# Down projections: the first four weight halves listed in TensorE's order; in the even layer the index weights become 16 more columns of the key tile

## The reference, cut to what matters

```python
x = x + (silu(gate) * val) @ w_down          # 2816 hidden -> 1024, in all four layers
```

```python
qa, ka, va, qb, kb, vb, qi, ki, wi = split_cols(h @ w_in_even[j], sizes_even)
...
rel = relu(einsum('bqhd,bsd->bqhs', qii, rmsnorm(ki)) * (64 ** -0.5))
score = einsum('bqhs,bqh->bqs', rel, wi * (16 ** -0.5))
```

## Time and profile before

| | |
|---|---|
| time, median of 3 runs | 1575.7 us (1574.05 to 1576.84) |
| profiled execution: its time, its span | 1576.8 us, 1574.8 us |
| TensorE busy | 1498.4 us, 95% of the span |
| VectorE, ScalarE, GpSimd busy | 65%, 52%, 19% |
| granted TensorE clock, mean | 0.988 |

### The profile page before, as it was taken

The page is one execution under the profiler, slowest core; times in us unless marked ns, Lnnn a source line. Parts: engine busy times, 40 slices in busy tenths (PEclk is TensorE's granted clock), DMA queues, the critical chain, the costliest instruction groups (busy, mean ns, idle before and its releaser), DMA issues.

```text
span 1574.8 us, 29754 instructions
## 1 busy us (share of the span) xinstructions
PE 1498.4 (95%) x12420; PEld 1417.7 (90%) x12420; DVE 1018.0 (65%) x1342; ACT 811.8 (52%) x1319; POOL 295.4 (19%) x190
## 2 busy tenths in 40 slices
PE   5999989999999999899999998989999999999997
PEld 2997879999999978799999997879999998899997
DVE  1785457787566854677546677667875655678854
ACT  3774355443347543554434545556654555566642
POOL 0002202997910032049000001100000001000000
PEclk9999999999999999999999999999999999999999
DMA  9455575665554365156435642244535543344442
GB/s 386 162 200 222 210 224 214 247 254 197 201 197 157 140 254 199 71 195 246 163 141 205 229 161 108 108 161 166 203 132 184 204 155 124 144 161 166 174 157 92
DMA packets 31926, 287.94 MB, mean 183 GB/s; under 512 B 3079, under 2 KB 11559, under 8 KB 12488
## 3 DMA queue, kind: packets, MB, share of 16 engines
q1 hardware_dynamic: 27400, 267.42, 46.0%
q0 software_dynamic: 2304, 16.78, 2.9%
q10 hardware_dynamic: 2112, 2.15, 0.5%
HBM read 285.23 MB, written 7.39 MB: 186 GB/s over the span
## 4 chain that ended last, share of the span: by engine, by line
PE 79%; DVE 9%; ACT 7%; issue 3%; DMA 1%; POOL 1%; SPq 0%; DVEq 0%; ACTq 0%
PE bank L656 22%; PE bank L657 22%; PE bank L658 22%; DVE w_lo L1972 3%; ACT w_hi L1456 2%; PE bank L974 1%; DMA ring<-ada 1%; PE bank L764 1%; PE bank L805 1%; PE bank L957 1%; PE bank L972 1%; PE bank L818 1%; PE bank L793 1%; PE bank L778 1%; DVE h L1937 1%
## 5 line engine op out<-in xcount | busy, mean ns | idle before, releaser
L656 PE MATMUL bank<-hi_T,w_hi 128*128 128x256 f32 x2184 | 625.8, 287 | 14.9 <-DVE h_lo L1957 7.5
L1972 DVE TENSOR_TENSOR w_lo<-ring,w_hi 128x2048 fp32r<-128x2048 f32 (+1 forms) x226 | 514.3, 2283 | 175.9 <-ACT w_hi L1456 174.2
L658 PE MATMUL bank<-hi_T,w_lo 128*128 128x256 f32 x2184 | 619.4, 284 | 0.0
L657 PE MATMUL bank<-h_lo,w_hi 128*128 128x256 f32 x2056 | 583.3, 284 | 0.0
L1456 ACT ACTIVATE w_hi<-ring 128x2048 fp32r<-128x2048 f32 (+1 forms) x226 | 391.8, 1735 | 264.9 <-PE bank L658 244.7
L656 PEld LDWEIGHTS bank<-hi_T,w_hi 128*128 128x128 f32 x2184 | 420.6, 193 | 23.2 <-issue 15.5
L658 PEld LDWEIGHTS bank<-hi_T,w_lo 128*128 128x128 f32 x2184 | 420.6, 193 | 0.0
L657 PEld LDWEIGHTS bank<-h_lo,w_hi 128*128 128x128 f32 x2056 | 396.4, 193 | 0.4 <-issue 0.2
L656 PE MATMUL bank<-act_hi,w_hi 128*128 128x256 f32 x704 | 201.4, 286 | 4.9 <-DVE w_lo L1972 4.9
L657 PE MATMUL bank<-act_lo,w_hi 128*128 128x256 f32 x704 | 200.7, 285 | 0.0
L658 PE MATMUL bank<-act_hi,w_lo 128*128 128x256 f32 x704 | 200.5, 285 | 0.0
(11 more groups left out here) (270 smaller groups left out, 1950.0 us busy)
## 6 DMA issues: line engine op xcount, KB each, us to landing
ring<-w_gu SPq DMA_DIRECT2D x22, 2048.0 KB, 7.7
ring<-w_dn SPq DMA_DIRECT2D x32, 1408.0 KB, 6.3
ring<-w_up SPq DMA_DIRECT2D x22, 2048.0 KB, 7.8
ring<-ada SPq DMA_DIRECT2D x16, 2048.0 KB, 8.6
ring<-w_mix SPq DMA_DIRECT2D x11, 2048.0 KB, 8.5
arena<-ada POOLq DMA_DIRECT2D x16, 1024.0 KB, 6.5
ring<-even_in SPq DMA_DIRECT2D x8, 2048.0 KB, 8.0
ring<-odd_in SPq DMA_DIRECT2D x6, 2048.0 KB, 8.0
```

The lines of the kernel that those rows point to most:

```text
L656: nc.tensor.matmul(out, wh, xh, start=start, stop=False)
L657: nc.tensor.matmul(out, wh, xl, start=False, stop=False)
L658: return nc.tensor.matmul(out, wl, xh, start=False, stop=stop)
L1972: V.tensor_tensor(w_lo[:, n % SLOTS, at], ring[:, n % SLOTS, at], w_hi[:, u % AHEAD, 0:size].bitcast(F32), ALU.subtract).then_inc(w_lo_rea ...
```

## The change

Part one: in each of the four down projections the list `halves` has its first four entries in the order (0,0), (1,0), (0,1), (1,1). ScalarE and VectorE split them in that order, and the places in `w_hi` and what `high` waits for follow. VectorE does the `low` of halves 3 and 4 before the first tile's residual, where it was half 3 before and half 4 behind it.

Part two: the tail has 80 columns (key once, then index weights) and is computed as one channel tile of 80 columns. ScalarE copies the 16 rows of index weights to `wi_rows` and the key's 64 rows to both partition halves of `qk2`. `turn_rows` gets two transposes that bring the index weights' tokens onto partitions, and VectorE copies them to `wi`. The tail takes one bank in place of three, and waits for `taken(2)`.

```diff
-TAILW = 144
+TAILW = HD + 16
...
-                 down=((1, 2), (2,)), tail=((1, 4), (2, 3, 4)), compress=((), ()))
+                 down=((1, 2), (2,)), tail=((1, 2), (2,)), compress=((), ()))
...
+        if kinds[0] == "down":
+            u = ph["u0"]
+            halves[u:u + 4] = [halves[u], halves[u + 2], halves[u + 1], halves[u + 3]]
...
+        wi_rows = pT[0:16, 0, 0, 0:S]
...
-                    u = ph["u0"] + 2 * j + part
+                    u = ph["u0"] + (j + 2 * part if j < 2 else 2 * j + part)
...
-            def turn_rows(l):
+            def turn_rows(l, weights=False):
 
                 pe.wait_ge(row_ready, l + 1)
+                if weights:
+                    pe.wait_ge(gemm_freed, phases["even"]["t0"])
+                    for qt in range(QT):
+                        nc.tensor.transpose(bank[:, 5, 16 + 16 * qt:32 + 16 * qt], wi_rows[:, qt * P:qt * P + P],
+                                            ident[0:16, 0:16])
...
                 for part in range(2):
                     half_in(h0 + 2 + part)
-                    w = split_half(h0 + 2 + part, TAILW)
                     if part == 0:
-                        taken(4)
-                    last = channel_tile(bank[:, WOVEN[4 % 3], 0:S], w, 0, (hi_T, h_lo), KT // 2 * part, KT // 2)
-                    if part == 1:
-                        last.then_inc(gemm_ready, 1)
-                    for qt in range(QT):
-                        last = token_tile(bank[:, WOVEN[(5 + qt) % 3], 0:16], w, P, P + 16, (hi_T, h_lo), qt,
-                                          KT // 2 * part, KT // 2)
-                        if part == 1 or qt == QT - 1:
-                            last.then_inc(gemm_ready, 1)
-                columns_half(4, 7)
-                turn_rows(0)
+                        taken(2)
+                    channel_tile(bank[0:TAILW, WOVEN[4 % 3], 0:S], split_half(h0 + 2 + part, TAILW), 0, (hi_T, h_lo),
+                                 KT // 2 * part, KT // 2, TAILW).then_inc(gemm_ready, 1)
+                columns_half(4, 5)
+                turn_rows(0, True)
...
-                take("tail", 0, qk2[:, 24, :], bank[:, WOVEN[4 % 3], 0:S])
-                for qt in range(QT):
-                    take("tail", 1 + qt, wi[:, qt, :], bank[:, WOVEN[(5 + qt) % 3], 0:16])
+                act.wait_ge(gemm_ready, phases["tail"]["tile_event"][0])
+                nc.scalar.activation(wi_rows, bank[HD:HD + 16, WOVEN[4 % 3], 0:S], ACT.Copy)
+                nc.scalar.activation(qk2[LO, 24, :], bank[LO, WOVEN[4 % 3], 0:S], ACT.Copy)
+                nc.scalar.activation(qk2[HI, 24, :], bank[LO, WOVEN[4 % 3], 0:S], ACT.Copy).then_inc(gemm_freed, 1)
...
                 dve.wait_ge(rows_turned, l + 1)
+                if l == 0:
+                    ch.mark(V.tensor_copy(wi, bank[:, 5, 16:48].rearrange("p (a n) -> p a n", a=QT)))
...
                 if each == 2:
                     low(ph["u0"] + AHEAD)
+                    low(ph["u0"] + 1 + AHEAD)
...
-                        if u < ph["u1"] - 1 and not (each == 2 and u == ph["u0"]):
+                        if u < ph["u1"] - 1 and not (each == 2 and u < ph["u0"] + 2):
                             low(u + AHEAD)
...
-        even_in=halved(even), even_tail=pack(np.concatenate([ki, ki, wi], axis=1)),
+        even_in=halved(even), even_tail=pack(np.concatenate([ki, wi], axis=1)),
```

More of the change, by code:

```diff
@@ L658, in three, with channel_tile @@
                 return nc.tensor.matmul(out, wl, xh, start=False, stop=stop)
-            def channel_tile(out, w, col, src, k0=0, ks=KT):
+            def channel_tile(out, w, col, src, k0=0, ks=KT, width=P):
                 (wh, wl), (xh, xl) = w, src
                 for k in range(ks):
-                    last = three(out, (wh[:, k, col:col + P], wl[:, k, col:col + P]), (xh[:, k0 + k, :], xl[:, k0 + k, :]),
-                                 k0 + k == 0, k0 + k == KT - 1)
+                    last = three(out, (wh[:, k, col:col + width], wl[:, k, col:col + width]),
+                                 (xh[:, k0 + k, :], xl[:, k0 + k, :]), k0 + k == 0, k0 + k == KT - 1)
                 return last
@@ L1243, in even_layer @@
                     .then_inc(ki_ssq, 1)
-                columns_half(5, 9)
-                columns_half(6, 11)
+                columns_half(5, 7)
+                columns_half(6, 9)
                 pe.wait_ge(ki_ready, 1)
-                taken(11)
+                taken(9)
                 index_scores(0)
                 index_scores(1)
-                columns_half(7, 13)
+                columns_half(7, 11)
                 index_scores(2)
                 index_scores(3)
-                tokens_half(8, 15)
+                tokens_half(8, 13)
                 index_scores(4)
                 index_scores(5)
-                tokens_half(9, 15)
+                tokens_half(9, 13)
                 index_scores(6)
                 index_scores(7)
-                columns_half(10, 17)
+                columns_half(10, 15)
                 pe.wait_ge(ix_relu, QT * 4)
-                taken(15)
+                taken(13)
                 pe.wait_ge(k_scaled, 2)
                 scores(u0)
-                columns_half(11, 19)
+                columns_half(11, 17)
                 scores(u0 + 1)
                 transposes(u0)
-                columns_half(12, 21)
-                taken(21)
+                columns_half(12, 19)
+                taken(19)
                 pe.wait_ge(k_scaled, 3)
@@ L1272, in even_layer @@
                 transposes(u0 + 1)
-                columns_half(13, 23)
+                columns_half(13, 21)
                 scores(u0 + 3)
@@ L1276, in even_layer @@
                 transposes(u0 + 2)
-                tokens_half(14, 25)
+                tokens_half(14, 23)
                 values(u0 + 2)
                 transposes(u0 + 3)
-                taken(25)
+                taken(23)
                 pe.wait_ge(k_scaled, 4)
                 scores(u0 + 4)
-                tokens_half(15, 25)
+                tokens_half(15, 23)
                 values(u0 + 3)
                 scores(u0 + 5)
-                columns_half(16, 27)
+                columns_half(16, 25)
                 transposes(u0 + 4)
-                columns_half(17, 29)
+                columns_half(17, 27)
                 values(u0 + 4)
@@ L1779, in columns @@
                 def columns(j, i, ts):
-                    two_taken("even", j, h0 + i, 7, ts)
+                    two_taken("even", j, h0 + i, 5, ts)
                 two_taken("first", 0, h0, 0, (16, 17))
@@ L1806, in even_layer @@
                 index_relu(5)
-                tokens_taken("even", 8, h0 + 9, 7, 0)
+                tokens_taken("even", 8, h0 + 9, 5, 0)
                 index_relu(6)
@@ L1823, in even_layer @@
                 exps(u0 + 4)
-                tokens_taken("even", 18, h0 + 15, 7, 1)
+                tokens_taken("even", 18, h0 + 15, 5, 1)
                 exps(u0 + 5)
```

## The result

The changed kernel takes 1562.4 us (median of 4, 1561.96 to 1563.13) against 1574.88 us before (median of 4 on the same chip). The ratio is 0.9914 (95% interval 0.9901 to 0.9927), or 13.5 us (11.5 to 15.6). A second measurement gave 1563.91 against 1576.4 us and 0.9918 (0.9903 to 0.9934), or 12.9 us. Forecast were 9.3. The direction and the places were right, the sum was some 4 us short: 1562.4 us is less than any outcome that the forecast named (A to D, 1564.6 to 1569.6), and only its allowance for the clock at other places, down to 1562.0, reaches it.

The account below looks back on a forecast made before the run. TensorE, busy 95% of the span, was taken to bound the kernel. Gains 6.4 (dn0) + 1.3 (down0, down1) + 1.6 (part two) = 9.3 us gave 1566.4 us, range 1562.0 to 1570.5.

Parts of the forecast that it names:

- A to D: A, the forecast: 1566.4, 0.62; B, lock replaces stall: 1569.6, 0.14; C, part two gives nothing: 1567.7, 0.10; D: 1564.6, 0.08.
- allowance for the clock at other places: Stalls of 1.4 to 1.9 us elsewhere may or may not lower the clock, 1.3 each, widening the range to 1562.0 to 1570.5.
- Both stalls: Dn0, TensorE's waits before (1,0) and (2,0): both go; each cost idle + 0.26 + 1.3 for clock, 3.4 and 3.3 us.
- 3.4 + 3.3 - 0.3 = 6.4: Dn0's gain in us: two stalls removed, less a new wait of 0.3.
- The third wait: Dn0, 0.60 idle before half 7, behind `low` after tile 2's residual: stays at 0.9 us, between 0 and 3.
- the new wait at half 6: Dn0, chunk 3 landing after 8.3 us, then `high` and `low`: 12.1 against 11.9 us, a wait of 0.2 to 0.3.
- The waits of 0.38 in down0 and down1: Before (1,0) in each: both go with the order, 2 x (0.38 + 0.26) = 1.3 us.
- ScalarE's wait for chunk 1: At half 1 of the down projections: in dn0 it delays ScalarE by 1.6 us, hidden; elsewhere the chunk lands earlier.
- rival F: All four down projections: ScalarE stands at half 1 for chunk 1, ahead of last copies; slower, 1580.6 us, chance 0.02.
- Such waits lower the clock ... I take 1.3: Even layer, new 2.8 us wait before h0+4: clock loss 1.3 us, bounds 0 and 2.6; part two gains 1.6.
- rival D: Clock stays up in part two (key's square binds, gain 2.5) and dn0's wait before half 7 goes: 1564.6, chance 0.08.
- nothing or the whole 2.0: Half 6 in dn0: under the port lock, the new wait is 0 or 2.0 us, depending on where L2655 falls.

Follow-up runs that it names:

- e2: Kernel before plus part two alone (80-column tail, down projections as before): 1573.11 us, ratio 0.9975.
- e1: Kernel before plus part one alone (new order of the first four halves in all four down projections): 1566.08 against 1575.98 us, ratio 0.9929.
- E5: Kernel before with GpSimd's modulation multiplications and sums beside the first two layers cut to 32 of 512 columns, loads kept: 1568.9 us in one execution.
- e14: Kernel before with the new order in down0 alone, second draw: 317.8 us from the even layer's end to the wait at 1368.
- e15: Kernel before, unedited, profiled a third time: span 1579.4 us.

## Why the forecast was short

**Part one, dn0: right in mechanism, mis-sized.** Both stalls went by the paths described, and nothing took their place. The forecast had 3.4 + 3.3 - 0.3 = 6.4; measured are 7.9 by the first pair of profiles and 6.3 to 7.9 over six profiles with the old order and GpSimd at work (209.9, 210.0, 210.0, 211.4, 211.5, 211.5 against 203.6), 7.1 in the mean. Three terms were off. The clock behind the first stall, counted as certain, dropped in three of six profiles; behind the second in all six; so 1.3 + 1.3 was some 0.7 too much. The third wait, left in at 0.9, went. The forecast gave its `low` 3.35 as the mean of two; the two took 4.06 and 2.71, and the first, half 7's, had met L2655 like those of halves 2 and 4: three of the shown `low`s had, not two. After the change GpSimd's multiplications come later against `low` of half 7, and it took 2.64. And the new wait at half 6, 0.3, wasn't there, because chunk 3 was issued ahead of GpSimd's load and landed in 6.5 us and not 8.3. Together these give 0.7 - 0.9 - 0.3: 0.5 us more gained than forecast, and by the measured mean 0.7.

**Part one, the others: right.** The waits of 0.38 in down0 and down1 went. ScalarE's wait for chunk 1 hid as said, and rival F never came near.

**Part two: the step that failed.** "Such waits lower the clock ... I take 1.3" charged the new kernel for its wait, and nothing to the kernel before, without a reason. The wait came as said (2.74) and lowered the clock in four of seven profiles, at 0.7 to 0.9. But the old tail did so in five of seven, with next to no wait, at 1.5 or 4.6 us. The profile on which the forecast rested was one of the two in which it hadn't. So part two is worth 3.9 in the mean of profiles and in e2's timing, against 1.6; 2.5 if the clock drops in neither kernel. The path was right: the tail in 2.8 us, then a wait ended by `low(h0+4)`. In the first pair of profiles both halves of rival D came true (clock up with a gain of 2.5, and the third wait gone); the forecast gave it 0.08 and 1564.6 us.

**What the forecast left out: some 2 us elsewhere.** The clock behind the 1.60 wait at 1310 dropped in all five profiles of the old arrangement and in none of the twelve others. It named such waits as noise ("may or may not lower the clock in a given run"). This one wasn't noise: it went one way with the change. Why, stays open. Of the 1.0 us in the last stretch 0.64 is down1's wait. The rest lies behind TensorE's last matmul: from the issue of the last output transfer to its landing, 2.1 us in place of 2.4. It goes with part two (e1's stretch is 206.0, e2's 206.4, the changed kernel's 205.7); why, is not shown.

The sum by the means of the unedited kernels' profiles from dn0 on (three each; dn0 and the tail by all that share them): 7.1 + 3.9 + 0.4 + 2.4 + 1.0, with 0.6 each of down0 and down1 in the last two terms, is 14.8 us. That leaves out dn1's stretch, which was 213.5 or 215.1 in either kernel, in the mean of three 0.5 longer after. The timings say 12.9 and 13.5, with intervals from 10.4 to 15.6.

On the shared port: the Trainium skill ("SBUF — State Buffer", SBUF: two separate sides) had been weighed as a reason to fear a new wait at half 6. E5 shows its weight, `low` at 1.63 with little work on GpSimd against 4.1 with all of it, on the side of the kernel before. At half 6 the forecast's reading of that rule, nothing or the whole 2.0, came out as nothing (`low` 1.62 to 1.72 in the nine profiles), and its middle value of 2.4 was wrong. The last section has what the traces show of the rule, and what it doesn't give.

## What to carry to other kernels

Where work is prepared by other engines, list it in the order in which the consumer takes it; a place that is freed by the last use of the wrong piece holds up all behind it. What such a stall costs was set here by a third engine, GpSimd: with little work on it the old order cost dn0 nothing. Cost the engine's clock on both sides of a change, with more than one profile of the kernel before: most waits repeat to 0.06 us, the clock doesn't. After a shortening, look at what TensorE now arrives at early: moving two small steps there gave another 1.5 us in the trace, and more in the timing.

## What the runs showed of the hardware that I had not expected

The granted clock fell at narrow matmuls almost without a wait. With 48 matmuls of 16 moving columns and a wait of 0.56 us, it went to 0.50 (1.2 GHz) in five of seven profiles, for 3 to 10 us, in e14 and e15 already during them: 0.21 us each instead of 0.11. TensorE was never idle for over 0.56 us there.

A wait of 1.80 us, in the same kernel at the same place, lowered the clock in three executions of six, one of 1.75 in six of six, one of 2.74 in four of seven, one of 1.60 in five of seventeen.

A VectorE subtraction of two SBUF operands (128 x 1408) took 1.62 us alone. In the 15 profiles with GpSimd at full work, between 370 and 470 us, 181 of them began while a GpSimd instruction was under way. In 162 the subtraction took as much longer as that instruction still had to run, less 0.1 us, 1.6 to 2.7 us in all, beside sums and beside multiplications alike; in one the next instruction went ahead as well (2.54). GpSimd then stood in its turn. Here, in the changed kernel, a `low` that began 0.10 us into a multiplication of 1.03 us, and the next multiplication:

```profile
384.40 2.41 DVE L1975 TENSOR_TENSOR w_lo<-ring,w_hi 128x1408 fp32r<-128x1408 f32 x1 [0.89 <-ACT w_hi L1458]
385.29 2.42 POOL L2661 TENSOR_TENSOR arena<-arena,c_silu 128x512 f32<-128x512 f32 x1
```

The other 18 are the `low`s of halves 2, 4 and 7 in the six profiles with the old order, at 4.0 to 4.2 us: there GpSimd did two more multiplications of 1.03 us before VectorE got its turn, though `low` had begun before them, as at 385.11 beside:

```profile
384.79 3.03 POOL L2655 TENSOR_TENSOR arena<-arena,c_silu 128x512 f32<-128x512 f32 x3
```

What decides between the two is not shown.
